# Last two down panels of an MLP in one accumulation, norms by pairs of tiles, and an epsilon column moved

## What is computed

```python
def swiglu(h, w_gu, w_down):
    g, u = jnp.split(h @ w_gu, 2, axis=-1)
    return (jax.nn.silu(g) * u) @ w_down

def sandwich(x, fn, g_pre, g_post, shift, scale, gate, res_w):
    h = modulate(rmsnorm(x, g_pre), shift, scale)
    y = rmsnorm(fn(h), g_post)
    return x + res_w * gate[:, None, :] * y
```

## Time and profile before

| | |
|---|---|
| median of three runs | 4009.24 us (4005.18 to 4013.02) |
| the profiled execution | 4013.02 us, its span in the profile 4010.8 us |
| PE busy | 3806.3 us of the span, mean granted clock 0.978 |
| DVE, ACT, POOL busy | 2153.8, 1373.4, 1483.8 us |
| first MLP's last product to the next stage's first, PE | 418.6 to 433.4 us |

### The profile page before, as it was taken

One profiled execution on the slowest core, in us unless ns is written; L12 is line 12 of the kernel. 1 busy time (PEld: TensorE's weight loads), 2 busy tenths in 40 slices (PEclk: granted clock), 3 DMA queues, 4 the chain that ended last, 5 costly groups with the idle time before them and its releaser, 6 DMA issues.

```text
span 4010.8 us, 50578 instructions
## 1 busy us (share of the span) xinstructions
PE 3806.3 (95%) x19252; PEld 3171.9 (79%) x19252; DVE 2153.8 (54%) x2983; ACT 1373.4 (34%) x1831; POOL 1483.8 (37%) x1012
## 2 busy tenths in 40 slices
PE   8999897999998999989999989999899999999999
PEld 7888685877886868878888778888687888777887
DVE  5555746136776371367732267777636368524334
ACT  3222644242223252373132342222425272334223
POOL 2555341435664302203333224444230305553443
PEclk9999998999999999999999999999899999999999
DMA  5555221224442101101221123333120202222222
GB/s 212 179 194 180 84 85 50 96 74 157 157 157 94 67 4 53 48 1 44 72 74 64 63 76 125 125 124 126 63 70 13 88 1 95 95 95 84 94 94 84
DMA packets 57658, 367.41 MB, mean 92 GB/s; under 512 B 5792, under 2 KB 12192, under 8 KB 14112
## 3 DMA queue, kind: packets, MB, share of 16 engines
q1 hardware_dynamic: 42064, 271.11, 19.8%
q10 hardware_dynamic: 15440, 94.12, 6.3%
HBM read 363.11 MB, written 2.10 MB: 91 GB/s over the span
## 4 chain that ended last, share of the span: by engine, by line
issue 61%; POOL 29%; PE 9%; POOLq 0%; DVE 0%; ACT 0%; DVEq 0%; ACTq 0%
POOL b_wlo L623 29%; PE ps L1838 3%; PE ps L1840 3%; PE ps L1839 3%; POOLq L637 0%; DVE b_y L1304 0%; POOLq L639 0%; DVE b_x L1308 0%; DVE b_y L1361 0%; PE ps L1914 0%; ACT b_whi L664 0%; PE ps L1901 0%; ACT b_xout L730 0%; DVE b_small L1306 0%; POOLq L623 0%
## 5 line engine op out<-in xcount | busy, mean ns | idle before, releaser
L623 POOL TENSOR_TENSOR b_wlo<-b_raw,b_whi 128x512 fp32r<-128x512 f32 x1008 | 1483.6, 1503 | 2506.5 <-ACT b_whi L664 2506.5
L1838 PE MATMUL ps<-b_hhi,b_whi 128*128 128x512 f32 x3032 | 1119.5, 369 | 22.6 <-POOL b_wlo L623 12.8
L1839 PE MATMUL ps<-b_hlo,b_whi 128*128 128x512 f32 x3032 | 1110.8, 366 | 0.0
L1840 PE MATMUL ps<-b_hhi,b_wlo 128*128 128x512 f32 x3032 | 1110.1, 366 | 0.0
L664 ACT ACTIVATE b_whi<-b_raw 128x2048 fp32r<-128x2048 f32 x252 | 481.4, 1910 | 903.2 <-PE ps L1840 878.6
L1838 PEld LDWEIGHTS ps<-b_hhi,b_whi 128*128 128x128 f32 x3032 | 574.5, 189 | 127.5 <-issue 23.9
L1839 PEld LDWEIGHTS ps<-b_hlo,b_whi 128*128 128x128 f32 x3032 | 574.8, 190 | 93.1 <-issue 1.4
L1840 PEld LDWEIGHTS ps<-b_hhi,b_wlo 128*128 128x128 f32 x3032 | 574.0, 189 | 93.5
L1361 DVE TENSOR_TENSOR b_y<-ps,b_y 128x512 f32<-128x512 f32 x496 | 335.6, 689 | 242.0 <-PE ps L1840 242.0
L1838 PE MATMUL ps<-b_whi,b_dhi 128*128 128x512 f32 x992 | 393.6, 397 | 0.1
L1840 PE MATMUL ps<-b_whi,b_dlo 128*128 128x512 f32 x992 | 393.4, 397 | 0.0
(11 more groups left out here) (308 smaller groups left out, 4776.7 us busy)
## 6 DMA issues: line engine op xcount, KB each, us to landing
b_raw<-panels SPq DMA_DIRECT2D x252, 1024.0 KB, 4.8
b_mraw<-mod_panels ACTq DMA_DIRECT2D x78, 1024.0 KB, 5.0
b_y<-mod_panels ACTq DMA_DIRECT2D x3, 1024.0 KB, 16.4
b_xin<-xT SPq DMA_DIRECT2D x1, 2048.0 KB, 26.0
b_mraw<-mod_panels SPq DMA_DIRECT2D x2, 1024.0 KB, 17.1
b_crow<-par ACTq DMA_DIRECT2D x2, 1024.0 KB, 5.0
b_rope<-rope ACTq DMA_DIRECT2D x4, 512.0 KB, 3.6
outT<-b_xout SPq DMA_DIRECT2D x4, 512.0 KB, 3.6
```

What stands on the lines that cost most here:

```text
L623: ins = pool.tensor_tensor(wlo[:, s, c], raw[:, s, c], whi[:, s, c].bitcast(F32), ALU.subtract)
L1838: pe.matmul(out, a[0], b[0], start=first, stop=False)
L1839: pe.matmul(out, a[0], b[1], start=False, stop=False)
L1840: return pe.matmul(out, a[1], b[0], start=False, stop=last)
```

## The change

The epsilon constant becomes column 82 of the tile small instead of a tile of its own. In each MLP the down products of the last two chunks are made together: for two token tiles (four PSUM tiles) at a time, PE multiplies with panel C-2, then with panel C-1 into the same PSUM tiles, and DVE adds once. The norm after an MLP takes tiles in pairs: post, post, pre, pre. ACT's split of the next stage's first panel moves into the norm, ahead of the last pair. The loops of ffn1, ffn2 and mlp1 have one trip less; their last two chunks, with their modulation panels, are straight code.

```diff
+    def rest_mods(self, c):
+        return self.mod0 + sum(self.lead) + (c - self.loop0) * self.half, self.half
...
-    small = sb("small", [82])
+    small = sb("small", [83])
...
-    eps = sb("eps", [1])
+    eps = small[:, 82:83]
...
-    MLPS = {"ffn1": Mlp("ffn1", True, L, first["ffn1"], 8, ((2, 2), 3, 4)),
-            "ffn2": Mlp("ffn2", True, L, first["ffn2"], 36, ((), 2, 5)),
-            "mlp1": Mlp("mlp1", False, TT, first["mlp1"], 56, ((0,), 2, 7)),
+    MLPS = {"ffn1": Mlp("ffn1", True, L, first["ffn1"], 8, ((2, 2), 3, 3)),
+            "ffn2": Mlp("ffn2", True, L, first["ffn2"], 36, ((), 2, 4)),
+            "mlp1": Mlp("mlp1", False, TT, first["mlp1"], 56, ((0,), 2, 6)),
...
+        if post and ORDER[ORDER.index(st) - 1] in MLPS:
+            for a in range(0, post[0] // P, 2):
+                out += [("post", a), ("post", a + 1)]
+                if pre:
+                    out += [("pre", a), ("pre", a + 1)]
+                if a == 0:
+                    out += [("pre", t) for t in early]
+            return out
...
             for c in m.rest:
-                units(c, m.panel(c))
+                units(c, m.panel(c), mods=m.rest_mods(c))
                 split(m.panel(c) + m.UP + 1)
-            split(m.p0 + m.UP * m.C + m.C)
             gate_rows(AFTER[st], (0, 1, 2, 3))
+            def before_tile(t):
+                if t == T // P - 2:
+                    split(m.p0 + m.UP * m.C + m.C)
+            return before_tile
...
                     if finish:
-                        while ready <= min(t + 1, post[0] // P - 1):
-                            finish(ready)
-                            ready += 1
+                        if t % 2 == 0:
+                            finish(t, 0)
+                        finish(t, 1)
...
                     dve.tensor_tensor(yt[:, t, :], yt[:, t, :], grow[:, group_of(t), :], ALU.mult).then_inc(*up("gated_y", (st, t)))
+                    if finish and t % 2 == 0:
+                        finish(t + 1, 0)
...
             for c in m.rest:
-                units(c)
-                for o in range(O):
+                units(c, mods=m.rest_mods(c))
+                for o in range(O if c < m.C - 1 else 0):
                     add(c - 1, o)
...
+            def down_part(c, p, o):
+                tok, half = slice(o // 2 * P, (o // 2 + 1) * P), o % 2
+                for k in range(2):
+                    ins = tri(ps[:, 4 + o % 4, :], (dhi[:, c % 2, k, tok], dlo[:, c % 2, k, tok]),
+                              wtile(p, 2, D, k, half * 512, 512), c == m.C - 2 and k == 0, c == m.C - 1 and k == 1)
+                return ins
+            def last_downs():
+                c, pa, pb = m.C - 2, down_panel(m, m.C - 2), down_panel(m, m.C - 1)
+                pe.wait_ge(lo_ready, pa + 1)
+                pe.wait_ge(*at("hid_lo", ("start", st), 2 * c + 2))
+                for o0 in range(0, O, 4):
+                    for o in range(o0, o0 + 4):
+                        prior = O * (c + 1) + o - 4 if o >= 4 else O * c + max(q for q in range(O) if q % 4 == o)
+                        pe.wait_ge(*at("added", ("start", st), prior + 1))
+                        ins = down_part(c, pa, o)
+                    if o0 == O - 4:
+                        ins.then_inc(panel_used, 1)
+                    if o0 == 0:
+                        pe.wait_ge(lo_ready, pb + 1)
+                        pe.wait_ge(*at("hid_lo", ("start", st), 2 * c + 4))
+                    for o in range(o0, o0 + 4):
+                        ins = down_part(c + 1, pb, o)
...
+                        if o == 1:
+                            gate_rows(AFTER[st], (0, 1, 2, 3))
...
-                down(c - 1, m.panel(c) + m.UP)
-            down(m.C - 1, m.p0 + (m.UP + 1) * m.C - 1)
+                if c < m.C - 1:
+                    down(c - 1, m.panel(c) + m.UP)
+            last_downs()
```

More of the change, by code:

```diff
@@ L1215, in _ @@
                 after_mix = ORDER[n - 1].startswith("mix")
-                norm(st, (lambda t, st=st: keep_half(st, t, 1)) if after_mix else None)
+                norm(st, (lambda t, st=st: keep_half(st, t, 1)) if after_mix else before_tile)
             elif st in MLPS:
-                mlp(MLPS[st])
+                before_tile = mlp(MLPS[st])
             else:
@@ L1292, in norm_stats @@
             post, pre = NORMS[st]
-            ready = 0
-            order = norm_order(st)
-            for what, t in order:
+            for what, t in norm_order(st):
                 if what == "post":
                     if finish:
-                        while ready <= min(t + 1, post[0] // P - 1):
-                            finish(ready)
-                            ready += 1
+                        if t % 2 == 0:
+                            finish(t, 0)
+                        finish(t, 1)
                     if t == 0:
@@ L1357, in add @@
                 else:
-                    dve.wait_ge(panel_used, lin(down_panel(m, c) + 1, m.per_trip, i))
+                    dve.wait_ge(panel_used, lin(down_panel(m, c if c < m.C - 2 else m.C - 1) + 1, m.per_trip, i))
                 dve.wait_ge(*at("added", ("start", st), lin(O * c + o + 1, 2 * O, i)))
@@ L1375, in mlp, with finish @@
             for c in m.rest:
-                units(c)
-                for o in range(O):
+                units(c, mods=m.rest_mods(c))
+                for o in range(O if c < m.C - 1 else 0):
                     add(c - 1, o)
             prepare(AFTER[st])
[L1381 to L1384, removed]
+            def finish(t, half):
+                add(m.C - 2, 2 * t + half)
+                if half:
+                    C.name("y", (AFTER[st], t), "added", C.count["added"])
             return finish
@@ L1989, in down @@
                         ins.then_inc(*up("down"))
-                    if c == m.C - 1 and o == 1:
-                        gate_rows(AFTER[st], (0, 1, 2, 3))
                 ins.then_inc(panel_used, 1)
+            def down_part(c, p, o):
[20 more added lines that the diff above has]
+                        ins = down_part(c + 1, pb, o)
+                        if o < O - 1:
+                            ins.then_inc(*up("down"))
+                        else:
+                            ins.then_inc(panel_used, 1)
+                        if o == 1:
+                            gate_rows(AFTER[st], (0, 1, 2, 3))
             first_ups()
```

## The result

| | before | after |
|---|---|---|
| median | 4009.24 us | 4020.10 us (4019.06 to 4025.69) |
| ratio to before | | 1.0027, interval 1.0019 to 1.0036: +10.8 us (+7.6 to +14.4) |
| span of the profiled execution | 4010.8 us | 4017.1 us |

The kernel became slower by a little more than a measurement can tell from no change. I had forecast 3999 us, a gain of a quarter of a per cent. The time lies inside the range of 3988 to 4032, on the other side of the kernel before.

The account below looks back on a forecast made before the run. TensorE, busy 95% of the span, bounds the kernel, except after each MLP, where the norm sets the pace. Terms 10.8 + 4.5 + 7.2 - 33 = -10.5 us from the median 4009.24 give 3999 us, range 3988 to 4032.

Parts of the forecast that it names:

- The epsilon column: Arena start moves to a multiple of 64 bytes, so 512-wide products of arena tiles step faster: -33 us, ends 0 and -34.
- rival 1: The 32 bytes of arena address do nothing, so only the MLP ends' cost remains: 4032 us, chance 0.26.
- rival 2: At arena products only one side's address counts: moving tile 4026 us, or weights 4005 us; chance 0.09.
- The new wait: At each MLP's end PE waits for the last down panel's low part: 3.6 us three times, 4.3 once, 15 us.
- The clock behind it: PE's granted clock falls behind three of the four low-part waits: 4.5 us in all, ends 0 and 12.
- MLP part: Cost at the four MLP ends, from stalls, clock, norm and POOL's clash together: 22.5 us.
- The norm by pairs: After each MLP, DVE's longer chain and waits for ACT: 10.8 us over four norms, the 15 us of stalls included.
- The clash with POOL: POOL's split slows the last pair's gate multiply and residual in each norm: 1.8 us each, 7.2 us, ends 0 and 14.
- Fewer adds, unrolled trips: Eight or twelve fewer adds per MLP and straight-code last trips are hidden by PE: nothing.

Follow-up runs that it names:

- MLP part alone: Kernel after with epsilon in a tile of its own again, so the arena lies where it was in the kernel before: 4027.68 us, ratio 1.0041.
- arena at 128: Kernel before with csil and epsilon moved into small of 96 columns, so the arena starts at a multiple of 128 bytes: 3980.98 us, ratio 0.9923.
- third phase: Kernel before with csil and epsilon in small padded to 104 columns, so the arena starts 32 bytes past a multiple of 128: 4008.77 us, ratio 0.9987.

## Why the prediction was wrong, point by point

- **The epsilon column: -33 forecast, -8.4 measured. This is the step that failed.** I saw two places, hhi/hlo fast and the arena slow, and wrote that the arena starts "32 bytes past a multiple of 64 today and at a multiple of 64 after". Two points give no unit: they fit 64 as well as 128. The sizes I summed held the warning, since hhi lies at a multiple of 128 and the arena after the change does not. That the start address sets the step, and the size of the gain, were right: 31 to 32 us came where the start was a multiple of 128. I had the larger unit as a clause of rival 1, priced at nothing. What happened lies between the forecast (to which I gave 0.62) and that rival (0.26): a part of the gain in each role, a case that I did not list.
- **"Moving tile or weights alone" (rival 2)** came nearest in its number by luck, 4026 us for the moving side alone against 4020. As a mechanism it is wrong: at 64 both roles gain, 0.0043 of 0.0067 us and 0.0008 of 0.0075.
- **The Trainium skill, TensorE: Matmul & The Clock Gate, § Back-to-back issue gap,** whose formula has no term for the operand's address, would make the move worth nothing. The runs speak against it here: the same 128x512 product steps by 0.2267 to 0.2342 us, depending on the start alone.
- **The new wait: 15 us forecast, 14.0 measured** (3.33 for 3.6 three times, 4.00 for 4.3), at the product, the tile and the releaser that the prediction named. Without it the kernel is 18.8 us faster, stall and clock together, where the prediction had 19.5.
- **The clock behind it: 4.5 forecast, about 4.6 in the profiled execution.** Three of four waits were followed by a fall. In the first, eight steps of 0.425 us instead of 0.233 make 1.5 us. The stretch from the last up product to the last down product shows it as well: 29.3 us in the first two MLPs and 27.8 in mlp2, where the clock stayed at 1.00. That it were three was a guess that came out: in the profiled execution of the MLP part alone all four waits were followed by a fall (granted clock 0.50 to 0.70 in the 3.8 us behind them), and the same stretch took 30.6 us in the first MLP.
- **The norm by pairs.** The waits for ACT came as worked out: 1.22 us three times for my 1.3, and 0.68 twice for 0.7. From the first gate multiply at 411.88 to the last tile at 435.65 DVE takes 23.8 us; I had 22.7 and a clash of 1.8, of which 1.1 came.
- **The clash with POOL: 7.2 forecast, 4.3 measured on DVE.** The place was right in all four norms, the size was not: the gate multiply lost 0.8 to 1.0 us (0.95 forecast), the residual only 0.22 (0.85). I had carried the loss over from the earlier trace rows as a price for each instruction. The rows of POOL's single subtractions show that it depends on when the instruction comes: the residual met 1.04 us of a running subtraction in the earlier trace rows (880.39 to 881.43), and 0.43 here (427.22 to 427.65). The Trainium skill, SBUF — State Buffer, § SBUF: two separate sides, says that of VectorE's instructions those with two inputs in SBUF, or in one of its two-port modes, contend with GpSimd. The rows agree on the first kind: the multiply and the residual slow down, the add with one input in PSUM does not. They also agree with the lock for a whole instruction that the prediction took from that section. Its 1.26 us, one whole subtraction, is the most that an instruction can wait by it; my estimate of 10 us took that for each, where the two met 0.98 and 0.43 us in the first of the norms.
- **Fewer adds, unrolled trips: nothing forecast.** No run has the merged products alone. Without the stall the whole MLP part takes the time of the epsilon column alone (-8.0 and -8.4 us), so that no gain from fewer adds is seen; but the norm by pairs alone adds 4.1 us to the ends, and with it and the clash in, the ends sum to the same (171.8 and 171.9). The earlier start that the merged products give the norm must bring about as much back, which is argued from these sums and not shown by a run.
- **Sum.** For the MLP part I had 22.5; the traces give 19.3 in the kernel after and 22.7 with the fast address. In the kernel after, with the three falls of the clock where they came, I had 6.1, 7.1, 4.6 and 4.7 us for the four ends; 5.3, 6.3, 3.8 and 3.9 came, each 0.8 less, and most of that is the smaller clash. With the arena at a multiple of 128 the whole change measured -8.8 us, and the prediction's sum from the median was -10.5. One term carried the sign, and only that term's condition was not met.

## What to carry to other kernels

When two operands of one shape run at different rates, write down their start addresses modulo several powers of two before pricing a move, and if the trace shows only two phases, price the case in which the move lands on a third. Merging two accumulations put matmuls that had covered a panel's way through two other engines behind the wait for that panel: before regrouping a stretch of TensorE, compare what is left ahead of a wait with the latency that runs beneath it. Where two engines hold each other up, the loss follows what is left of the one's running instruction when the other's comes, so that a loss seen in one place is no fixed price for another. And the slow helper must be moved to where the other side reads elsewhere (here, adds from PSUM), and not merely later.

## What the runs showed of the hardware

Step of consecutive 128x512 fp32r products in us, by where the one operand starts in bytes past a multiple of 128 (the other starts at one):

| past | arena tile moving (ch) | arena tile as weights (dhi) | run |
|---|---|---|---|
| 0 | 0.2268 | 0.2270 | arena at 128 |
| 32 | 0.2334 | 0.2332 | third phase |
| 64 | 0.2291 | 0.2334 | kernel after |
| 96 | 0.2334 | 0.2342 | kernel before |

That 64 is better than 32 for a moving tile and not for weights, I had not expected, and what in the chip makes it is open. At 256 columns the order is another. The mean of one product with ch at 64 is 277 ns in the kernel after, below the 283 of before and the 281 with the arena at 128, and its unbroken runs step by 0.113 to 0.118 us where they took 0.120 before and 0.119 with the arena at 128. So a multiple of 128 is not the best start for every shape. The kernel after, then the arena at 128:

```profile
L1855 PE MATMUL ps<-b_ch,b_whi 128*128 128x256 f32 x112 | 31.0, 277 | 0.0
```

```profile
L1838 PE MATMUL ps<-b_ch,b_whi 128*128 128x256 f32 x112 | 31.5, 281 | 0.0
```
